# A transformer layer pair on one core: the first projections in two Strassen blocks per pair, and weight sums made by adding DMAs

## The chip, the cores and the metric

The kernel runs on one core of a Trainium2 chip (trn2). The metric is the device time of one launch in microseconds, lower is better. The kernel before takes 2067.45 us (median of three runs, 2067.3 to 2068.65).

## What is computed

Two transformer blocks over 256 tokens of width 2048, batch 1, all in float32. Cut to what matters here:

```python
h = rmsnorm(x, norm_mix_g)
proj = h @ w_in                        # 2048 x 6144: queries, keys, values, retention, its gate
x = x + concat(diff_attention(...), retention(...) * silu(rg)) @ w_o
x = x + cross_attention(rmsnorm(x, norm_x_g) @ w_xq, hm @ w_xk, hm @ w_xv) @ w_xo
x = x + (silu(hf @ w_gate) * (hf @ w_up)) @ w_down
# second block: h2 = rmsnorm(rmsnorm(x)) * (1 + scale) + shift, scale and shift from silu(c) @ w_ada
proj2 = h2 @ w_in_2                    # windowed attention, pooling, their gates
g = sigmoid(h2 @ w_merge + b_merge)
out = x + gate * rmsnorm((g_a * (y_a @ w_br_attn) + g_p * (y_p @ w_br_pool)) @ w_out)
```

## The kernel before

All large products have 256 tokens (two tiles of 128) on one side and a weight on the other. A **panel** is 512 columns of a weight. Its rows come in chunks of 512, each in two halves of 256 rows; a half (256 x 512, as 128 partitions x 1024 floats, 512 KB) is one **item**. An item is loaded by a DMA from SyncE's queue into one of eight places of `raw` (`RAWS = 8`). ScalarE then rounds it to float32r (`whi`, line 1718) and VectorE writes what the rounding left out (`wlo`, line 2494). TensorE multiplies with the activations, split in the same way, in three passes: high by high, high by low, low by high (lines 1117 to 1119), each one matmul of 128x128 stationary and 512 columns. One such split weight is an **entry**. Entries go through a ring of four (`HALVES = 4`): entry n is split when TensorE has finished entry n-4. A normal entry serves both token tiles and costs TensorE 12 matmuls.

Panels are worked on in **pairs** (f, s). The first 512 rows of a pair, called a block here, are done by Strassen's scheme in Winograd's form: seven products M1 to M7 in place of eight, each one token tile, so 6 matmuls. M5, M6, M7 and M4 need a sum or a difference of two items, which VectorE makes in place in `raw` (`sum_weights`, line 2507): M5 = b12 + b11, M6 = b22 + M5's sum, M7 = b11 - M6's sum, M4 = b21 + M6's sum. Activations are summed once per 512 rows (`make_forms`, lines 1819 to 1830). The panels of the first projection are named tq, v and rg; they meet the chunks x0 to x3 of x. After two single panels tq0 and tq1 come the five x pairs (v0, tq2), (tq3, v1), (tq4, tq5), (v2, rg0), (v3, rg1), then o, xk, xv, xq, xo; g with u, and d or e; kv alone; q with ga, pu with gp; m; ba, bp; out.

The order of everything is fixed when the program is built. `Stream` writes the list of steps, entries and items; `_slots` says how many entries are split before each step; `_loads` sorts the items by first use and gives each a place, the one whose last user comes soonest. SyncE issues the loads in that order, each waiting until its place is taken over by its last user. ScalarE and VectorE walk the same list of steps, and between entries take one piece of `jobs` (attention, norms, transposes) where a step allows it. GpSimd (POOL) issues the small loads and computes the roots of the norms (line 2547), strictly in the order of its program. `X`, 16 KB a partition, holds the rows of x: loaded at the start from POOL's queue (line 2579), squared by ScalarE for the norm (line 1148), and next used when `o` adds to it.

```python
for form, n in (("M5", at["M5"] - early), ("M6", at["M3"] + 1), ("M7", at["M1"] + 2),
                ("M4", max(at["M2"], at["M6"]) + 1)):
    self.sums_before[n] = at[form]     # before entry n is split, VectorE makes this sum
```

Of the kernel before, what the change touches and what calls it, by code (L numbers as in the profile page):

```python
# [9 lines left out]
F32 = mybir.dt.float32  # L10
F32R = mybir.dt.float32r
ALU = mybir.AluOpType
# [56 lines left out]
def layouts(v):  # L69
# [10 lines left out]
Entry = namedtuple("Entry", "item add minus nth")  # L80

Step = namedtuple("Step", "n p c hf tiles form start end made job taken snap aside")
# [8 lines left out]
FORMS = ("x", "mix", "mem", "hx", "xo", "hf", "h0", "h4", "h8", "mod", "mg")  # L91
TURNED = ("mix", "hx", "xo", "hf", "h0", "h4", "h8", "mg")

# [12 lines left out]
    "raw0", "raw1", "raw2", "raw3", "raw4", "raw5", "raw6", "raw7", "hi", "lo", "hi_first", "lo_first", "half", "t0_end", "ada",  # L106
# [12 lines left out]
    "x_hi", "x_lo", "mem_g", "mem_hi", "mem_lo", "st_hi", "a_hi", "a_lo", "af", "forms", "f_hi", "f_lo",  # L119

    "t_sum", "snap", "snap_v", "pre", "fin", "gated", "hh",
# [101 lines left out]
class Stream:  # L223
# [14 lines left out]
    def __init__(self, groups):  # L238
# [4 lines left out]
        self._done, self._set, self.sums = 0, 1, 0  # L243

        self.aside_at, self.ahead = {}, {}
        self.sums_before = {}
# [16 lines left out]
        self.last_of_item, self.last_sum_of = {}, {}  # L263
        for n, entry in enumerate(self.entries):
            self.last_of_item[entry.item] = n
            if entry.add is not None:
                self.last_sum_of[entry.add] = entry.nth
# [14 lines left out]
    def _entry(self, item, add=None, minus=False):  # L282
        if add is not None:
            self.sums += 1
        self.entries.append(Entry(item, add, minus, self.sums))
        return len(self.entries) - 1

    def _step(self, n, p, c, hf, tiles, form=None, start=False, end=False, job=True, taken=True, snap=None,
              aside=None):
        self.steps.append(Step(n, p, c, hf, tiles, form, start, end, None, job, taken, snap, aside))  # L290
        if end:
            self.end[p] = n + 1
# [21 lines left out]
    def _pair(self, f, s):  # L314
# [3 lines left out]
        b22, b12, b11, b21 = (self._item(*which) for which in ((f, 0, 1), (f, 0, 0), (s, 0, 0), (s, 0, 1)))  # L318
        todo = iter([(c, hf) for c in range(1, chunks) for hf in range(2)])
        at = {}  # L320
# [5 lines left out]
        def product(form, place, add=None, minus=False, **more):  # L326
            at[form] = n = self._entry(place, add, minus)
            panel, tile, _, half, _ = PRODUCTS[form]
            self._step(n, (f, s)[panel], 0, half, (tile,), form, **more)

        product("M5", b12, b11, start=True, job=False)
        product("M3", b22, start=True, job=False)
        normal(f, *next(todo), snap=("s5", q))
        product("M1", b11, start=True, job=False)
        if chunks == 4:
            normal(f, *next(todo), snap=("s1", q))
            product("M6", b22, b12)
            product("M2", b21, start=True, snap=("v", q))
            normal(f, *next(todo))
            normal(f, *next(todo))  # L340
        else:
            product("M2", b21, start=True, snap=("s1", q))
            product("M6", b22, b12)
            normal(f, *next(todo), snap=("v", q))
        product("M7", b11, b22, minus=True)
        normal(f, *next(todo), snap=("s3", q))
        product("M4", b21, b22, aside=q)
        for c, hf in todo:
            normal(f, c, hf)
        todo = {"u": self._early, "d": self._early, "m": self._late}.get(self.panels[s].kind, [])  # L350
        for i, (c, hf) in enumerate((c, hf) for c in range(1, chunks) for hf in range(2)):
# [3 lines left out]
        self.pairs.append(((f, s), at))  # L355

        early = 1 if self.panels[f - 1].stagger == "first" else 2
        for form, n in (("M5", at["M5"] - early), ("M6", at["M3"] + 1), ("M7", at["M1"] + 2),
# [2378 lines left out]
```

## Time and profile before

| | |
|---|---|
| runs, median of 3 | 2067.45 us |
| profiled execution, span | 2065.9 us |
| time around the span, as the median less the span | 1.5 us |
| TensorE busy, 9334 matmuls | 2054.4 us, 99% |
| VectorE / ScalarE / GpSimd busy | 1667.2 (81%) / 1181.2 (57%) / 50.0 us (2%) |
| TensorE in the chain that ended last | 95% |
| DMA engines, weight loads (queue q1) | 432.07 MB, 62.9% of their time |
| DMA engines, GpSimd's queue (q0) | 19.94 MB, 3.0% |
| granted TensorE clock | full in nearly all of the span |

The profiled execution has no time of its own beside its span. Busy shares are means over stages. A DMA's time "to landing" goes from its issue to the last of its sixteen signals. "Idle before" is an engine's own idle time ahead of an instruction, with what ended it. Matmuls overlap, so the mean duration of one (390 ns) is not the distance between two.

### The profile page before, as it was taken

What the parts mean: (1) busy time and instruction counts of PE and PEld (TensorE: products, weight loads), DVE (VectorE), ACT (ScalarE), POOL (GpSimd) and SP (SyncE); (2) the same over time, 40 slices, a digit from 0 to 9 for tenths busy, and PEclk for the clock granted to TensorE, in tenths of its full rate; (3) what the DMA queues carried; (4) which work ended last, traced back from release to release, by engine and by line L of the source; (5) the groups of instructions that cost most, each with busy time, mean ns of one, the idle gap of its engine ahead of it and who ended that gap; (6) DMA issues with size and microseconds to landing.
All of it is one profiled execution on the core that took longest, in us unless ns stands there. A gap on an engine that the chain in (4) does not pass through costs nothing.

```text
span 2065.9 us, 25348 instructions
## 1 busy us (share of the span) xinstructions
PE 2054.4 (99%) x9334; PEld 1699.8 (82%) x9334; DVE 1667.2 (81%) x1830; ACT 1181.2 (57%) x1533; POOL 50.0 (2%) x84
## 2 busy tenths in 40 slices
PE   9999999999999999999999999999999999999998
PEld 8888888888888888888888888888788888888787
DVE  6877778867766788989889898898777778988875
ACT  7666557656655565555555555555756655654453
POOL 1000000000000000000000000000000000000000
PEclk9999999999999999999999999999999999999999
DMA  9555557655544458777777777776465567789763
GB/s 347 180 172 184 184 180 259 225 182 184 189 158 153 159 185 300 267 259 242 243 237 259 261 242 243 236 270 213 158 214 178 180 201 234 269 285 329 219 197 109
DMA packets 219259, 453.74 MB, mean 220 GB/s; under 512 B 14449, under 2 KB 17153, under 8 KB 219009
## 3 DMA queue, kind: packets, MB, share of 16 engines
q1 hardware_dynamic: 213232, 432.07, 62.9%
q0 software_dynamic: 5616, 19.94, 3.0%
q8 instruction: 74, 1.21, 0.2%
q14 instruction: 49, 0.39, 0.1%
q10 hardware_dynamic: 288, 0.13, 0.0%
HBM read 447.88 MB, written 4.19 MB: 219 GB/s over the span
## 4 chain that ended last, share of the span: by engine, by line
PE 95%; DVE 2%; ACT 1%; issue 1%; DMA 1%; POOL 0%; SPq 0%; DVEq 0%; POOLq 0%; ACTq 0%
PE ps L1117 30%; PE ps L1119 30%; PE ps L1118 29%; PE ps L687 2%; DVE wlo L2494 1%; PE ps L837 1%; PE ps L817 1%; PE ps L921 0%; DMA FR<-in_post_norm_g_dram 0%; PE ps L952 0%; PE ps L963 0%; PE ps L901 0%; DMA FR<-in_x_t_dram 0%; ACT whi L1718 0%; DVE raw L2507 0%
## 5 line engine op out<-in xcount | busy, mean ns | idle before, releaser
L2494 DVE TENSOR_TENSOR wlo<-raw,whi 128x1024 fp32r<-128x1024 f32 x835 | 1010.4, 1222 | 262.8 <-ACT whi L1718 257.4
L1718 ACT ACTIVATE whi<-raw 128x1024 fp32r<-128x1024 f32 x835 | 876.6, 1058 | 564.5 <-PE ps L1119 518.2
L1117 PE MATMUL ps<-whi,bh 128*128 128x512 f32 x1384 | 547.3, 395 | 2.3 <-DVE wlo L2494 2.1
L1119 PE MATMUL ps<-whi,bl 128*128 128x512 f32 x1384 | 539.9, 390 | 0.0
L1118 PE MATMUL ps<-wlo,bh 128*128 128x512 f32 x1384 | 539.2, 390 | 0.0
L1117 PE MATMUL ps<-whi,ah 128*128 128x512 f32 x1080 | 429.3, 398 | 0.2 <-DVE wlo L2494 0.2
L1119 PE MATMUL ps<-whi,al 128*128 128x512 f32 x1080 | 421.6, 390 | 0.0
L1118 PE MATMUL ps<-wlo,ah 128*128 128x512 f32 x1080 | 420.9, 390 | 0.0
L1117 PEld LDWEIGHTS ps<-whi,bh 128*128 128x128 f32 x1384 | 260.1, 188 | 57.0 <-DVE wlo L2494 3.1
L1119 PEld LDWEIGHTS ps<-whi,bl 128*128 128x128 f32 x1384 | 259.8, 188 | 54.7
L1118 PEld LDWEIGHTS ps<-wlo,bh 128*128 128x128 f32 x1384 | 260.2, 188 | 52.5 <-issue 0.2
L1117 PEld LDWEIGHTS ps<-whi,ah 128*128 128x128 f32 x1080 | 202.9, 188 | 43.1 <-issue 1.3
L1119 PEld LDWEIGHTS ps<-whi,al 128*128 128x128 f32 x1080 | 202.8, 188 | 43.1
L1118 PEld LDWEIGHTS ps<-wlo,ah 128*128 128x128 f32 x1080 | 203.1, 188 | 41.5 <-issue 1.0
L2507 DVE TENSOR_TENSOR raw<-raw 128x1024 f32<-128x1024 f32 x160 | 195.6, 1223 | 15.7 <-DVE wlo L2494 15.7
L2108 DVE SCALAR_TENSOR_TENSOR FR<-raw,Z,FR 128x1024 f32<-128x1024 f32 x90 | 115.2, 1280 | 0.0
L1221 ACT ACTIVATE side<-ps 128x512 f32<-128x512 f32 x120 | 70.7, 589 | 16.3 <-PE ps L1119 16.3
L1117 PE MATMUL ps<-whi,fbh 128*128 128x512 f32 x184 | 73.9, 402 | 0.0
L1119 PE MATMUL ps<-whi,fbl 128*128 128x512 f32 x184 | 71.9, 391 | 0.0
L1118 PE MATMUL ps<-wlo,fbh 128*128 128x512 f32 x184 | 71.8, 390 | 0.0
L1835 DVE TENSOR_TENSOR FR<-ps,side 128x512 f32<-128x512 f32 x81 | 53.2, 685 | 7.7 <-PE ps L1119 7.7
L1117 PE MATMUL ps<-whi,fah 128*128 128x512 f32 x136 | 55.1, 405 | 0.0
(264 smaller groups left out, 1334.6 us busy)
## 6 DMA issues: line engine op xcount, KB each, us to landing
raw<-in_w_in_dram SPq DMA_DIRECT2D x168, 512.0 KB, 4.5
raw<-in_w_ada_dram SPq DMA_DIRECT2D x96, 512.0 KB, 4.6
raw<-in_w_gate_dram SPq DMA_DIRECT2D x88, 512.0 KB, 4.9
raw<-in_w_up_dram SPq DMA_DIRECT2D x88, 512.0 KB, 5.4
raw<-in_w_down_dram SPq DMA_DIRECT2D x88, 512.0 KB, 5.4
raw<-in_w_merge_dram SPq DMA_DIRECT2D x64, 512.0 KB, 5.0
raw<-in_w_o_dram SPq DMA_DIRECT2D x32, 512.0 KB, 4.8
raw<-in_w_xk_dram SPq DMA_DIRECT2D x32, 512.0 KB, 4.7
```

Source lines behind the costliest of these rows:

```text
L687: ins = e.transpose(T[b].ap[:, kk * 256 + t * 128:kk * 256 + t * 128 + 128], src[:, t, (2 * b + kk) * 128:(2 * b + kk + 1) * 128], ident[: ...
L817: ins = e.matmul(A[0].ap[:, t * S:(t + 1) * S], QTC[:, d, t * 128:(t + 1) * 128], XKT[:, 4 * h + d, :], start=(d == 0), stop=(d == 3))
L837: ins = e.matmul(A[b].ap[:, dd * S:(dd + 1) * S], XV[:, k, c0:c0 + 128], PTC[:, k, :], start=(k == 0), stop=(k == 1))
L1117: e.matmul(o, xh[:, k, tokens], wh, start=first, stop=False, skip_group_check=more)
L1118: e.matmul(o, xh[:, k, tokens], wl, start=False, stop=False, skip_group_check=more)
L1119: ins = e.matmul(o, xl[:, k, tokens], wh, start=False, skip_group_check=more, stop=kk == 1 and (st.end or st.form in READ))
L1221: done(e.activation(side_of(pair[place[0]], place[1]), bank_of(pair[panel], t)[:, :], ACT.Copy), "snap")
L1718: done(e.activation(split_at(n)[0], place(item), ACT.Copy), "hi")
L1835: return e.tensor_tensor(dst, src, side_of(p, t), side_op(p))
L2108: done(e.scalar_tensor_tensor(acc, src, csilu[:, k:k + 1], acc, ALU.mult, ALU.add), "ada")
L2494: done(e.tensor_tensor(lo, place(stream.entries[n].item), hi.bitcast(F32), ALU.subtract), "lo")
L2507: done(e.tensor_tensor(place(item), place(add), place(item), ALU.subtract if minus else ALU.add), "t_sum")
```

## The change

1. In the five x pairs two blocks (1024 of the 2048 rows) are done by Strassen's scheme (`QUADS`), with the products of both spread over the pair. Chunk x1 gets its own sums of activations (`x1`).
2. In the pairs named in `QUEUED` the sums are no longer VectorE's, but DMAs from GpSimd's queue that add one item to another in SBUF (`accum_op=ALU.add`, after.py line 2692): M5 and M4 of a pair with one block, M5, M6 and M4 of both blocks in the x pairs. Differences (M7), and all sums of g, u, d, e and m, stay on VectorE.
3. The table of places counts such a sum as in use for three entries longer (`LANDING = 3`).
4. From the end of tq1 to the end of rg1, `X` gives four more places (`SPARES = 4`); SyncE waits with the first of these loads until x has been squared, and x is loaded again before `o` needs it.

```diff
+QUADS = {"tq": 2, "v": 2, "rg": 2}
+QUEUED = ("tq", "v", "rg", "o", "xk", "xv", "xq", "xo", "q", "ga", "pu", "gp", "out")
+SPARES = 4
+LANDING = 3
...
+        else:
+            product("M5", 0, start=True, job=False)
+            product("M5", 1, job=False)
+            product("M3", 0, start=True)
+            normal(f, *next(todo), snap=("s5", q))
+            product("M3", 1, job=False)
+            product("M1", 0, start=True, job=False)
+            product("M1", 1)
             normal(f, *next(todo), snap=("s1", q))
...
+            product("M2", 0, start=True, job=False)
+            product("M6", 0)
+            product("M6", 1)
             normal(f, *next(todo), snap=("v", q))
...
+            product("M2", 1, job=False)
+            product("M7", 0)
+            product("M7", 1)
+            normal(f, *next(todo), snap=("s3", q))
+            product("M4", 0, aside=q)
...
             normal(s, c, hf)
...
+            if quads == 2 and i == 0:
+                product("M4", 1)
...
+        queued = self.panels[f].kind in QUEUED
+        early = 2
+        if self.panels[f - 1].stagger == "first":
+            early = 3 if queued else 1
+        elif queued:
+            early = 1 if q == 0 else 6
+        for k, made in enumerate(at):
+            for form, n in (("M5", made["M5"] - early), ("M6", made["M3"] + 1),
+                            ("M7", made["M1"] + 2 if quads == 1 else made["M6"] + 1),
+                            ("M4", max(made["M2"], made["M6"]) + 1)):
+                self.sums[made[form]] = Sum(n, made, k, form, queued and form in (("M5", "M4") if quads == 1 else ("M5", "M6", "M4")))
...
+        for m, one in self.sums.items():
+            for item in (self.entries[m].item, self.entries[m].add):
+                used(item, (one.before, 1))
+                used(item, (one.before + (LANDING if one.queue else 0), 1))
...
+        def ready_to_sum(e, m):
+
+            made, form = stream.sums[m].pair, stream.sums[m].form
+            if form == "M5":
+                for item in stream.entries[m]:
+                    e.wait_ge(*loaded(item))
+            else:
+                e.wait_ge(*sum_done(made["M5" if form == "M6" else "M6"]))
+                e.wait_ge(s["lo"], made[{"M6": "M3", "M7": "M1", "M4": "M2"}[form]] + 1)
...
+                while queued and stream.sums[queued[0]].before <= n:
+                    m = queued.pop(0)
+                    item, add = stream.entries[m]
+                    ready_to_sum(e, m)
+                    e.dma_start(place(item), place(add), accum_op=ALU.add).then_inc(sum_done(m)[0], 16)
...
+            add_weights(stream.end[index["rg", 1]] - 1)
+            for item in stream.last_in_spare.values():
+                wait_taken(e, item)
+            load_x()
...
+                elif stream.place[i] >= RAWS:
+                    e.wait_ge(s["x_sq"], 8)
```

`wait_taken` waits for the sums that read or write an item as well as for its last split. ScalarE waits for the sum's own signal before it splits the entry.

GpSimd's program at the start, from the root of the first norm (line 2547) and the load of the attention bias `c_bias` on. Before:

```order
L2547 TENSOR_TENSOR Z<-Z 128x2 [waits s_ms]
L2587 DMA FR<-in_c_bias_dram 128x1536
L2547 TENSOR_TENSOR Z<-Z 128x2 [waits s_ms] x4
```

and now:

```order
L2654 TENSOR_TENSOR Z<-Z 128x2 [waits s_ms]
L2712 DMA FR<-in_c_bias_dram 128x1536
L2692 DMA raw<-raw 128x1024 [waits s_raw0,s_raw7]
L2692 DMA X<-X 128x1024 [waits s_raw9,s_raw8]
L2692 DMA X<-raw 128x1024 [waits s_lo,s_sum_m5a]
L2692 DMA raw<-X 128x1024 [waits s_lo,s_sum_m5b]
L2692 DMA raw<-X 128x1024 [waits s_lo,s_sum_m6a]
L2692 DMA raw<-raw 128x1024 [waits s_lo,s_sum_m6b]
L2692 DMA X<-raw 128x1024 [waits s_raw7,s_raw11]
L2692 DMA raw<-X 128x1024 [waits s_raw8,s_raw3]
L2654 TENSOR_TENSOR Z<-Z 128x2 [waits s_ms]
```

The six sums of the first x pair (M5, M6, M4, each for both blocks) and the M5 of the next stand between the bias load and the next root; the first of them has the bias load ahead of it in the queue.

VectorE from the eviction of tq0 (line 1896 before, 2002 now) on, where the first x pair's M5 is made. Before:

```order
L1896 TENSOR_SCALAR FR<-ps,Z 128x512 [waits s_r,s_half]
L2507 TENSOR_TENSOR raw<-raw 128x1024 [waits s_raw7,s_raw6]
L2494 TENSOR_TENSOR wlo<-raw,whi 128x1024 [waits s_hi] x3
L1878 COPY FR<-ps 128x512 [waits s_t1_full]
L2494 TENSOR_TENSOR wlo<-raw,whi 128x1024 [waits s_hi]
```

and now:

```order
L2002 TENSOR_SCALAR FR<-ps,Z 128x512 [waits s_r,s_half]
L2604 TENSOR_TENSOR wlo<-raw,whi 128x1024 [waits s_hi] x3
L1984 COPY FR<-ps 128x512 [waits s_t1_full]
L2604 TENSOR_TENSOR wlo<-X,whi 128x1024 [waits s_hi]
```

The sum (line 2507) is gone from VectorE; its result is now waited for by ScalarE ahead of the third of these splits, and the M5 of the second block is the one read from `X`. Over the program TensorE has 8580 rows in place of 8610, VectorE 854 splits in place of 839 and 120 sums in place of 160, and GpSimd 60 adding DMAs.

## Rows read from the trace of the kernel before

**Rows 1.** The page: chain that ended last, by engine and by line.

```profile
PE 95%; DVE 2%; ACT 1%; issue 1%; DMA 1%; POOL 0%; SPq 0%; DVEq 0%; POOLq 0%; ACTq 0%
```

**Rows 2.** Waits of TensorE: us in total, times, longest.

```profile
PE ps L1117 <- DVE wlo L2494: 2.3, 4, 1.0
```

**Rows 3.** Timeline of TensorE, 540 to 548 us: start, duration; 37 matmuls.

```profile
539.67 0.39 PE L1119 MATMUL ps<-whi,al 128*128 128x512 f32 x1
...
547.83 0.39 PE L1119 MATMUL ps<-whi,al 128*128 128x512 f32 x1
```

**Rows 4.** Groups of instructions: the splits and the sums.

```profile
L2494 DVE TENSOR_TENSOR wlo<-raw,whi 128x1024 fp32r<-128x1024 f32 x835 | 1010.4, 1222 | 262.8 <-ACT whi L1718 257.4
L1718 ACT ACTIVATE whi<-raw 128x1024 fp32r<-128x1024 f32 x835 | 876.6, 1058 | 564.5 <-PE ps L1119 518.2
L2507 DVE TENSOR_TENSOR raw<-raw 128x1024 f32<-128x1024 f32 x160 | 195.6, 1223 | 15.7 <-DVE wlo L2494 15.7
```

**Rows 5.** Timeline of TensorE at the waits near 348 and 1504 us.

```profile
348.54 0.50 PE L1117 MATMUL ps<-whi,bh 128*128 128x512 f32 x1 [0.74 <-DVE wlo L2494]
...
1504.41 0.47 PE L1117 MATMUL ps<-whi,bh 128*128 128x512 f32 x1 [0.33 <-DVE wlo L2494]
```

**Rows 6.** The chain that ended last, same two places: start, us, what.

```profile
334.98 1.22 DVE raw L2507
...
1495.94 1.22 DVE raw L2507
```

**Rows 7.** The x pairs, 53 to 290 us: busy by engine, clock, DMA share.

```profile
53.00:290.00 237.00, 236.79 (x1092) 196.34 (x1091) 183.89 (x226) 144.23 (x212) 4.71 (x7) 1.00 0.58 184
```

**Rows 8.** DMA queues and issues in 53 to 290 us.

```profile
q1 hardware_dynamic: 22082, 42.57, 56.8%
...
raw<-in_w_in_dram SPq DMA_DIRECT2D x72, 512.0 KB, 4.3
```

**Rows 9.** All DMA issues from GpSimd's queue of 512 KB: median us to landing.

```profile
X<-in_x_dram POOLq DMA_DIRECT2D x4, 512.0 KB, 9.5
FR<-in_mem_t_dram POOLq DMA_DIRECT2D x4, 512.0 KB, 9.4
...
FR<-in_w_pool_group_dram POOLq DMA_DIRECT2D x2, 512.0 KB, 6.4
FR<-in_c_mg_dram POOLq DMA_DIRECT2D x2, 512.0 KB, 7.4
```

**Rows 10.** Line 2579, the four loads of x issued in a row.

```profile
DMA to landing us min/median/max: 7.6/9.5/11.5
```

**Rows 11.** Timeline of GpSimd, 20 to 43 us.

```profile
20.72 3.04 POOL L2579 DMA_DIRECT2D X<-in_x_dram  x4 [19.75 <-DMA raw<-in_w_in_dram]
...
41.37 0.73 POOL L2547 TENSOR_TENSOR Z<-Z 128x2 f32<-128x2 f32 x1 [13.90 <-DVE Z L1767]
42.06 0.60 POOL L2587 DMA_DIRECT2D FR<-in_c_bias_dram  x1
```

**Rows 12.** DMA queues, 46 to 48 us; then the issue of c_bias.

```profile
q0 software_dynamic: 112, 0.68, 83.8%
q1 hardware_dynamic: 80, 0.15, 19.9%
...
FR<-in_c_bias_dram POOLq DMA_DIRECT2D x1, 768.0 KB, 7.3
```

**Rows 13.** TensorE at the first x pair, its M5; ScalarE and VectorE on M5's split.

```profile
52.79 0.39 PE L1117 MATMUL ps<-whi,fah 128*128 128x512 f32 x1
...
45.26 1.05 ACT L1718 ACTIVATE whi<-raw 128x1024 fp32r<-128x1024 f32 x1
...
44.01 3.57 DVE L2494 TENSOR_TENSOR wlo<-raw,whi 128x1024 fp32r<-128x1024 f32 x3
```

**Rows 14.** Waits of VectorE in 53 to 290 us.

```profile
DVE wlo L2494 <- ACT whi L1718: 30.9, 33, 1.7
...
DVE FR L2012 <- POOL Z L2547: 3.3, 4, 0.9
```

More of the change, by code:

```diff
@@ L77 @@
 Panel = namedtuple("Panel", "kind i w col rows stagger")
-Entry = namedtuple("Entry", "item add minus nth")
-Step = namedtuple("Step", "n p c hf tiles form start end made job taken snap aside")
+Entry = namedtuple("Entry", "item add")
+Step = namedtuple("Step", "n p c hf tiles form quad start end made job taken snap aside")
+Sum = namedtuple("Sum", "before pair quad form queue")
+Spare = namedtuple("Spare", "first last")
 PRODUCTS = {"M3": (0, 0, True, 1, 0), "M5": (0, 1, True, 1, 1), "M1": (1, 1, False, 0, 0),
@@ L266, in __init__ @@
             if entry.add is not None:
-                self.last_sum_of[entry.add] = entry.nth
+                self.sums_of.setdefault(entry.add, []).append(n)
+        self.sum_order = sorted(self.sums, key=lambda m: self.sums[m].before)
+        self.sum_signal, used = {}, {}
+        for m in self.sum_order:
+            one = self.sums[m]
+            name = f"sum_{one.form.lower()}{'ab'[one.quad]}" if one.queue else "sum_w"
+            used[name] = used.get(name, 0) + 1
+            self.sum_signal[m] = name, used[name] * (16 if one.queue else 1)
+        self.spares = [Spare(self.end_of["tq", 1], self.end_of["rg", 1])] * SPARES
         self._places()
@@ L346, in _pair, with product @@
[L346 to L349, printed above, removed]
+        def product(form, k, start=False, **more):
+            b22, b12, b11, b21 = places[k]
+            item, add = {"M5": (b12, b11), "M3": (b22, None), "M1": (b11, None), "M6": (b22, b12), "M2": (b21, None),
+                         "M7": (b11, b22), "M4": (b21, b22)}[form]
+            at[k][form] = n = self._entry(item, add)
+            panel, tile, _, half, _ = PRODUCTS[form]
+            self._step(n, (f, s)[panel], k, half, (tile,), form, k, start=(start and k == 0), **more)
@@ L1729, in scalar_program @@
                 jobs.start(job)
+            for job in (pause(8), make_forms("x1")):
+                aside.start(job)
             for i, st in enumerate(stream.steps):
@@ L1823, in make_forms @@
                 after_own(done(e.tensor_tensor(a11, a22, a11, ALU.subtract)))
[L1824 removed]
+                done(e.tensor_tensor(a12, a12, a11, ALU.add), summed)
                 yield
@@ L2489, in make @@
                         add_ada(item)
-                    if n in stream.sums_before:
-                        sum_weights(stream.sums_before[n])
+                    for m in [m for m in stream.sum_order if stream.sums[m].before == n and not stream.sums[m].queue]:
+                        sum_weights(m)
                     hi, lo = split_at(n)
@@ L2496, in sum_weights @@
             def sum_weights(n):
[L2498 to L2507 removed]
+                item, add = stream.entries[n]
+                ready_to_sum(e, n)
+                done(e.tensor_tensor(place(item), place(add), place(item),
+                                     ALU.subtract if stream.sums[n].form == "M7" else ALU.add), "sum_w")
             done(e.memset(tbl[:, :], 0.0), "tbl_zero")
@@ L2517, in vector_program @@
                 jobs.start(job)
+            for job in (pause(8), make_forms("x1")):
+                aside.start(job)
             for i, st in enumerate(stream.steps):
```

202 lines of the change are left out of this document (121 added, 81 removed).

## The prediction

> **What bounds the kernel now.** I read the chain that ended last first: TensorE holds 95% of it [rows 1]. Then what TensorE waits for: VectorE's splits, four times, 2.3 us in all [rows 2]. So the time is the number of matmuls times the distance between two. The timeline gives that distance: 37 matmuls start within 547.83 - 539.67 = 8.16 us, so 0.227 us each at the full clock [rows 3]. A product (6 matmuls) is 1.36 us of TensorE, a normal entry (12) 2.72. VectorE and ScalarE have room: both wait for the ring before a split, VectorE 262.8 us in all and ScalarE 564.5 [rows 4]. In the x pairs VectorE is busy 184 of 237 us and still waits 30.9 us for ScalarE's halves of the splits [rows 7, 14]. The DMA engines are busy 58% there [rows 7]. A matmul less is therefore worth its full 0.227 us; a sum less on VectorE is worth something only where TensorE waits for it; and a new wait costs only what is left of it after the ring of four entries has run empty.
>
> **Matmuls, certain.** Each x pair does seven products for eight once more: 6 matmuls less, 5 pairs, 30 in all, which is what TensorE's rows say (8610 to 8580). 30 x 0.227 = **-6.8 us**. The clock stays full, since TensorE stays busy.
>
> **Splits and sums.** 15 more entries cost ScalarE 15 x 1.06 and VectorE 15 x 1.22 us, and 40 sums less give VectorE 40 x 1.22 back [rows 4]. In the x pairs the balance on VectorE is 15 x 1.22 - 10 x 1.22 = +6.1 us over some 230 us, beside 53 us in which it was idle [rows 7]: that costs nothing as long as the ring hides it (below). In the other stages 30 sums leave VectorE. That gains where a sum stood in the chain. Two of TensorE's waits qualify: at 348.54 (0.74 us) and at 1504.41 (0.33 us) [rows 5]; each chain goes back through VectorE without a gap worth naming to an M5 sum (334.98, 1495.94) [rows 6], which takes 1.22 us, more than either wait. Both M5 move to the queue with several entries of lead. **-1.1 us.** The other waits come from the norm between the layers and stay.
>
> **The x1 forms** (4 scalings, 4 small sums, one split on each side) run between entries of tq1, where TensorE does not wait. Nothing; without cover some 3 us of VectorE would be late once.
>
> **The adding DMAs.** No row shows one. Nearest are GpSimd's loads of the same size: medians 6.4 to 9.5 us to landing [rows 9], 7.6 when first and 11.5 when last of four in a row [rows 10]. Below: how much data moves per time. In 46 to 48 us queue q0 alone took 83.8% of the engines for 0.68 MB, so 0.52 MB takes 0.838 x 2 x 0.52/0.68 = 1.3 us of all sixteen [rows 12]. If the sum reads its target too, twice that, 2.6. An estimate for a lone sum is 6.4 to 9.5 plus 0 to 1.3, so 6.4 to 10.8, middle 8 us. The Trainium skill says why reading might count double: an adding transfer issues two source reads per chunk on the same ring, and its rate halves (Collectives: The Full Stack, The bandwidth ceiling); no row here can show it.
>
> What the program allows: the second block's M6 sum is asked for when that block's M3 is split. From the moment M3's slot is free (TensorE has finished the entry four before it) until TensorE starts M6 there are 7 products and 2 normal entries, 7 x 1.36 + 2 x 2.72 = 15.0 us. Off go 2.3 us for M6's own split (as for the first M5, from 45.26 to 44.01 + 3.57 = 47.58 [rows 13]) and 2.6 for M3's, the same and 0.3 for the signals. That leaves **10.1 us**. The same sum for the second M4, and for M4 in pairs with one block, leaves 11.4; the first block's M6 has 12.8. M5 has six entries of lead. So a sum of 8 us is hidden; only the far end of the range, or a burst like the four loads, is not.
>
> The load on the DMA engines: q1 took 56.8% of 237 us for 42.57 MB [rows 8]. The 30 sums of the x pairs add 39 to 78 us to 137, so a share of 0.75 to 0.92. Loads land in 4.3 us [rows 8]; they get slower, but are due 7 us or more ahead of use by the table, with four more places. Nothing in the sum; up to 3 us in the range.
>
> Here a rule speaks. The skill's fit for a DMA from GpSimd's queue is 2.0 us plus bytes / 436e3 (DMA: Bandwidth & Descriptors, Anatomy of one DMA): 3.2 us for one item. The rows say 6.4 and more for the same size, so the trace disagrees and I don't use it. By the page no sum could be late, and the result would be the best case below.
>
> **The first x pair, the place that costs.** Its M5 has no lead. GpSimd works in order: root at 41.37, c_bias at 42.06 to 42.66 [rows 11], then M5 of block one. c_bias lands at 42.06 + 7.3 = 49.4 [rows 12], and the sum's data follow it on the same queue. TensorE starts that M5 at 52.79 [rows 13]; VectorE's sum was done nearly 9 us before [rows 13]. The second sum follows on the queue at once, if its two items (which wait for x to be squared, about 41 us) are there by then. Bounds: each takes 1.3 us after the one ahead (landing 50.7 and 52.0), or, at the pace of the four x loads in the same rush, (11.5 - 7.6)/3 + 0.73 = 2.0 us doubled for the second read (53.4 and 57.4). I take 2.6 us, the data rate above with two reads: 52.0 and 54.6. The split adds 2.3. So the first M5 is ready at 54.3, 1.5 us late; the second at 56.9 where TensorE comes free at 54.3 + 1.36 = 55.7, 1.2 late. **+2.7 us** (low 0.2, high 5.6). Behind ScalarE's wait stand its evictions and snapshots, which nobody needs sooner.
>
> **Products in a row.** Before, three entries in a row always held a normal one, 5.44 us; now M3 M1 M1, M2 M6 M6 and M2 M7 M7 take 4.08. A split takes 2.6 us from a free slot to ready, so 1.5 us is left for jobs in between, and a job's burst on VectorE is 2 to 3 us. Each such place can cost 0 to 1 us, 15 to 20 places; most are caught up by the normal entry ahead. I take **+1.0 us** in all, bounds 0 and 4.
>
> **Moved waits.** x is reloaded (2 MB, 4 issues of 0.73 us each) when the last spare place is free, some 20 us ahead of `o`'s first use and 11.5 us long at worst [rows 10]: hidden. Roots: VectorE waits for one 3.3 us over four heads [rows 14]; an issue of a sum ahead of it adds 0.7 at most, in VectorE's slack.
>
> **Sum.** -6.8 - 1.1 + 2.7 + 1.0 = -4.2 us. Against the profiled span that is 2065.9 - 4.2 = 2061.7; the median of the runs stands 1.5 us over that span, so **2063.2 us** against 2067.45. A measurement can tell about 0.2% of this kernel, 4.1 us, from no change; the forecast lies just at that edge, on the side of faster.
>
> **The rivals.**
> *A, the forecast or better:* 2063.2, down to 2067.45 - 6.8 - 1.1 + 0.2 = 2059.7 if the sums are cheap and nothing is late. For it: TensorE is the bound, and the matmuls are gone for certain. Chance 0.44.
> *B, paid back in place:* the first pair costs its high end, 5.6, and the rows of products 2 us: 2067.45 - 7.9 + 7.6 = 2067.1. For it: c_bias is ahead of the sums, and the engines are full when they come, 83.8 and 19.9% [rows 12]. Chance 0.34.
> *C, slower: sums land behind their window in every x pair.* Decisive is the landing of the second block's M6: above 10.1 us ScalarE's wait empties the ring, and each us over is one of TensorE's, for M6 and, above 11.4, again for M4. At 12.8 us (11.5 as in rows 10, plus a second read of 1.3) that is 2.7 + 1.4 = 4.1 us per pair, 20.5 in five; with the first pair's 5.6 and 1.0 for products 2067.45 - 7.9 + 27.1 = 2086.7; at 11.4 us 6.5 + 5.6 + 1.0 - 7.9, so 2072.7. For it: queue q0 was never used beside busy loads in this stage but for single transfers, and the engines go from 58 to 75 or 92%. Against it: lone transfers land in 6.4 to 7.4. A way to get there is GpSimd itself, which would have to issue while VectorE works 78% of the time. The four x issues took 3.04 us, 0.76 each, and c_bias 0.60 [rows 11], so no row shows a hold-up. The skill says that VectorE with two inputs in SBUF contends with GpSimd's reads, but not with the writing of descriptors (SBUF — State Buffer, Who interferes with whom); by that, the trace agrees and this way is closed. Chance 0.22.
> That the matmuls aren't saved is excluded by the rows of TensorE.
>
> **How the numbers follow.** Faster by over 0.2% (below 2063.3) is A: 0.44. Within 0.2% (2063.3 to 2071.6) is B with the mildest part of C: 0.34. Slower is the rest of C: 0.22. The range starts at 2059, just under the best case, and reaches into C to 2075, a landing near 11.6 us; beyond it lies some 0.15. The own range of A and B is 2059.5 to 2068.
>
> **What will show it.** The three matmul lines count 30 less. TensorE waits near 53 and 56 us for wlo, 1.5 and 1.2 us; the waits at 348 and 1504 are gone. The adding DMAs show 6.4 to 10.8 us to landing, q0's share grows by 60 x 1.3 to 2.6 us, 4 to 8% of the span, and ScalarE waits for them in few places. Wrong would be: TensorE waits for VectorE in every x pair by more than 1 us (C), no wait at 53 us (A's best case), or sums that take over 12 us.

## The result, and the profile after

The changed kernel takes 2082.81 us (median of four runs, 2082.58 to 2086.58) against 2067.95 of the kernel before in the same session: a ratio of 1.0074, 95% interval [1.0062, 1.0086]. It is slower by 15 us, beyond the range of the forecast (2059 to 2075). Its profiled execution has a span of 2080.6 us, 14.7 over that of before. Two kernels below (e9 and e12) each had one execution far out of line (3470 and 7460 us, with a granted clock of 0.56 and 0.27), from which nothing is read.

The page of the changed kernel, busy time and chain; the groups that answer to [rows 1, 4] (splits L2604 and L1818):

```profile
PE 2052.0 (99%) x9304; PEld 1693.9 (81%) x9304; DVE 1642.5 (79%) x1810; ACT 1198.7 (58%) x1553; POOL 105.4 (5%) x148
...
q1 hardware_dynamic: 213232, 432.07, 61.4%
q0 software_dynamic: 14832, 53.50, 11.8%
...
PE 90%; DVE 4%; ACT 2%; issue 2%; DMA 2%; SPq 0%; POOL 0%; DVEq 0%; POOLq 0%; ACTq 0%
```

TensorE lost its 30 matmuls (9334 to 9304 records), VectorE has less to do, and yet TensorE's share of the chain falls from 95 to 90%. Its waits, against 2.3 us for VectorE's splits [rows 2]:

```profile
PE ps L1213 <- issue: 6.5, 2, 3.8
PE ps L1213 <- DVE wlo L2604: 4.8, 5, 1.7
PE ps L1213 <- DVE side L1961: 2.8, 3, 1.4
PE ps L1213 <- ACT side L1318: 2.8, 2, 2.3
PE ps L782 <- ACT FR L1307: 2.0, 2, 1.1
PE ps L1154 <- POOL ones L2648: 1.0, 1, 1.0
PE ps L845 <- DVE FR L2110: 0.8, 1, 0.8
```

**Where the time went.** TensorE's matmuls of lines 1213 to 1215 run in the order of the program, so the start of each panel can be compared with that of the kernel before. This table has the difference in us (positive: later than before) for this and all kernels below, each from one profiled execution. A step from one column to the next is what that stretch cost; "a pair costs" means such a step below, and the first pair's goes from tq1 to tq3, because a late M5 already delays the start of v0. Two executions of one kind differ by some 0.5 us at the start. The five x pairs lie between v0 and o0 (v0, tq3, tq4, v2 and v3 are their first panels, o0 the panel behind them); each should have given 1.36 us.

```
                              tq1   v0  tq3  tq4   v2   v3   o0  xk0  xk2  ga0   end
the change                    1.4  5.3 11.1 11.8 12.8 14.6 14.5 13.5 16.2 15.3  14.7
e1_first_m5_vector            1.5  1.5  2.4  3.1  4.1  5.9  5.8  4.8  8.8  8.0   7.3
e2_one_block                  0.5  5.2 10.5 10.5 10.5 10.5 10.5  9.6 13.8 12.9  12.2
e3_sums_on_vector             1.7  1.7  3.0  7.5 10.9 15.2 19.5 19.5 19.5 19.6  19.4
e4_mem_ahead                  1.8  5.8 13.1 13.8 14.8 16.7 16.5 15.5 17.0 16.1  16.2
e5_copy_not_add               2.1  5.3 11.5 12.2 13.2 15.0 14.9 13.9 14.3 13.6  12.9
e6_bias_behind                1.6  4.1 12.9 13.5 14.6 16.4 16.3 15.3 19.5 18.7  18.0
e7_loads_held                 1.8  1.7  7.9  8.6  9.6 11.4 11.3 10.3 12.8 12.1  11.9
e8_three_mended               0.4  0.4  2.0  2.7  3.7  5.6  5.5  4.4  6.3  5.4   4.8
e9_difference_first           0.1  0.1  1.7  1.6  1.5  3.3  2.1  1.1  3.1  2.2   1.6
e10_m7_later                  0.7  0.7  2.3  3.0  4.4  8.0  7.9  6.9  8.8  7.9   7.3
e11_both                      0.1  0.1  1.7  1.5  1.9  2.6  1.4  0.4  2.1  1.2   0.7
e12_one_block_mended          0.9  0.9  0.9  0.9  1.0  1.0  1.0 -0.0  1.6  0.7   0.0
e13_two_blocks_xk_vector      0.1  0.0  1.6  1.5  1.9  2.6  1.3  0.3  0.3 -0.6  -1.2
e14_one_block_xk_vector       0.2  0.1  0.2  0.2  0.2  0.2  0.2 -0.8 -0.8 -1.4  -2.0
e15_two_blocks_last_pair      0.2  0.1  0.4  0.4  0.5  0.5 -0.2 -0.5 -0.5 -1.3  -2.0
e16_two_blocks_no_landing     0.2  0.2  1.7  1.6  2.0  3.5  2.3  1.3  2.8  1.9   1.3
```

In the change 1.4 us go at the start, 9.7 in the first x pair (that is 11.1 with the 1.36 it should have given), 3.4 in the other four (8.9 with theirs), 2.7 between xk0 and xk2; 1.0, 0.9 and 0.6 us come back at three places (in o, up to the q pairs, before out).

A step of this table holds both TensorE's waits and what the clock took behind them, and the second differs from execution to execution. For the first pair the two can be told apart (waits in 50 to 72 us; granted clock as the mean over 57 to 71 us; the clock's price is an estimate, half of TensorE's busy time while the granted clock was at half, 1.2 GHz). That price is part of the first column:

```
                            pair costs   waits   clock 57-71   price of the clock
the change                        9.7     6.8      0.88          1.4
e1_first_m5_vector                0.9     0.0      1.00          0.0
e2_one_block                     10.0     6.3      0.76          3.4
e4_mem_ahead                     11.3     6.2      0.63          4.0
e5_copy_not_add                   9.4     4.9      0.76          3.4
e6_bias_behind                   11.3     4.5      0.51          5.8
e7_loads_held                     6.1     3.2      0.88          1.7
```

**The first pair.** TensorE there, the last matmul before the gap and those behind it (start, duration, idle before):

```profile
53.93 0.39 PE L1215 MATMUL ps<-whi,al 128*128 128x512 f32 x1
58.07 0.77 PE L1213 MATMUL ps<-whi,fah 128*128 128x512 f32 x1 [3.75 <-issue]
...
60.34 0.63 PE L1215 MATMUL ps<-whi,fal 128*128 128x512 f32 x1
61.31 0.47 PE L1213 MATMUL ps<-whi,bh 128*128 128x512 f32 x1 [0.34 <-DVE wlo L2604]
...
65.66 0.47 PE L1213 MATMUL ps<-whi,fah 128*128 128x512 f32 x1 [2.72 <-issue]
```

and ScalarE, which waits for the two M5 sums:

```profile
55.66 1.06 ACT L1818 ACTIVATE whi<-raw 128x1024 fp32r<-128x1024 f32 x1 [9.38 <-DMA raw<-raw]
58.85 1.06 ACT L1818 ACTIVATE whi<-X 128x1024 fp32r<-128x1024 f32 x1 [2.14 <-DMA X<-X]
61.62 0.20 ACT L1420 ACTIVATE Z<-Z 128x2 f32<-128x2 f32 x1 [1.72 <-DVE Z L2077]
61.85 1.28 ACT L1422 ACT_TABLE_LOAD   x1
...
63.26 1.04 ACT L1818 ACTIVATE whi<-X 128x1024 fp32r<-128x1024 f32 x1
```

The sums were issued at 43.61 and 47.60 us and landed 12.0 and 11.2 us later. The releaser "issue" of TensorE's two long waits says only that the profile inferred none; ScalarE's rows give it. The first wait is for the sum. The second (2.72 us, at 65.66) is for the next split, which ScalarE begins at 63.26 because one of its jobs, waiting for VectorE, stands between it and the sums' splits. The windows say why the sums were late (behind the five engines' busy times, PE, PEld, DVE, ACT, POOL: granted clock, DMA share, GB/s). Before:

```profile
50.00:54.00 4.00, 4.00 (x20) 3.30 (x19) 2.80 (x7) 3.57 (x6) 0.00 (x0) 1.00 0.33 124
54.00:58.00 4.00, 4.00 (x19) 3.31 (x18) 4.00 (x5) 3.01 (x4) 0.00 (x0) 1.00 0.80 257
58.00:62.00 4.00, 4.00 (x21) 3.33 (x20) 2.76 (x4) 2.98 (x4) 0.00 (x0) 1.00 0.44 137
```

and now:

```profile
50.00:54.00 4.00, 4.00 (x20) 3.23 (x18) 0.00 (x0) 0.00 (x0) 0.00 (x0) 1.00 1.03 263
54.00:58.00 4.00, 0.32 (x2) 0.00 (x0) 1.26 (x2) 1.06 (x1) 0.00 (x0) 0.94 1.05 264
58.00:62.00 4.00, 3.59 (x9) 2.46 (x10) 2.36 (x7) 1.41 (x3) 0.00 (x0) 0.63 1.05 404
...
53.00:290.00 237.00, 221.59 (x1003) 179.52 (x1002) 184.20 (x234) 156.28 (x223) 30.01 (x36) 0.99 0.86 244
```

In 50 to 54 us the DMA engines were at 0.33 and are now full, as they are from 44 to 65 us. SyncE issues nine loads in 42 to 49 us, the first four into the new spare places; before it issued three in 40 to 47. With c_bias and two sums that read and write, all of it stands in line: c_bias lands at 52.8 us (before: 49.4), the sums 2.9 and 6.1 us behind it. Over the five pairs the share rose from 0.58 [rows 7] to 0.86, inside the 0.75 to 0.92 forecast; in this stretch the mean says nothing.

### The profile page after: what moved, and what is told of

Read it like the earlier page. It is cut to its first block, busy times and chain, and to the rows that moved or that the text cites. A ratio compares the mean times of both kernels' runs of the same rounds, so it can differ in the third digit from the quotient of the medians.

```text
span 2080.6 us, 25310 instructions
## 1 busy us (share of the span) xinstructions
PE 2052.0 (99%) x9304; PEld 1693.9 (81%) x9304; DVE 1642.5 (79%) x1810; ACT 1198.7 (58%) x1553; POOL 105.4 (5%) x148
## 3 DMA queue, kind: packets, MB, share of 16 engines
q0 software_dynamic: 14832, 53.50, 11.8%
## 4 chain that ended last, share of the span: by engine, by line
PE 90%; DVE 4%; ACT 2%; issue 2%; DMA 2%; SPq 0%; POOL 0%; DVEq 0%; POOLq 0%; ACTq 0%
PE ps L1213 28%; PE ps L1215 28%; PE ps L1214 28%; DVE wlo L2604 2%; PE ps L782 2%; ACT whi L1818 1%; PE ps L932 1%; PE ps L912 1%; ACT junk L1244 1%; DMA X<-X 1%; DMA FR<-in_mem_dram 1%; DMA FR<-in_x_t_dram 0%; PE ps L1016 0%; PE ps L1058 0%; PE ps L1047 0%
## 5 line engine op out<-in xcount | busy, mean ns | idle before, releaser
L2604 DVE TENSOR_TENSOR wlo<-raw,whi 128x1024 fp32r<-128x1024 f32 x811 | 979.9, 1220 | 300.4 <-ACT whi L1818 295.6
L1818 ACT ACTIVATE whi<-raw 128x1024 fp32r<-128x1024 f32 x811 | 850.6, 1057 | 556.0 <-PE ps L1215 481.8
L1213 PE MATMUL ps<-whi,bh 128*128 128x512 f32 x1424 | 563.3, 396 | 1.5 <-DVE wlo L2604 1.4
L1215 PE MATMUL ps<-whi,bl 128*128 128x512 f32 x1424 | 555.1, 390 | 0.0
L1214 PE MATMUL ps<-wlo,bh 128*128 128x512 f32 x1424 | 554.4, 389 | 0.0
L1213 PE MATMUL ps<-whi,ah 128*128 128x512 f32 x1030 | 409.8, 398 | 6.3 <-DVE wlo L2604 3.5
L1215 PE MATMUL ps<-whi,al 128*128 128x512 f32 x1030 | 401.8, 390 | 0.0
L1214 PE MATMUL ps<-wlo,ah 128*128 128x512 f32 x1030 | 401.1, 389 | 0.0
L2610 DVE TENSOR_TENSOR raw<-raw 128x1024 f32<-128x1024 f32 x114 | 139.2, 1221 | 5.5
L2692 POOL DMA_DIRECT2D raw<-raw x43 | 38.5, 910 | 597.1 <-DVE wlo L2604 539.3
```

What stands on the lines that cost most here:

```text
L1213: e.matmul(o, xh[:, k, tokens], wh, start=first, stop=False, skip_group_check=more)
L1214: e.matmul(o, xh[:, k, tokens], wl, start=False, stop=False, skip_group_check=more)
L1215: ins = e.matmul(o, xl[:, k, tokens], wh, start=False, skip_group_check=more, stop=kk == 1 and (st.end or st.form in READ))
L1818: done(e.activation(split_at(n)[0], place(item), ACT.Copy), "hi")
L2604: done(e.tensor_tensor(lo, place(stream.entries[n].item), hi.bitcast(F32), ALU.subtract), "lo")
L2610: done(e.tensor_tensor(place(item), place(add), place(item), ALU.subtract if stream.sums[n].form == "M7" else ALU.add), "sum_w")
```

## The experiments

Each kernel is compared with the kernel before on the same chip; ratios have their 95% interval. Diffs are against the changed kernel.

### The first pair's sums on VectorE

```diff
-  Sum(n, made, k, form, queued and form in (("M5", "M4") if quads == 1 else ("M5", "M6", "M4")))
+  Sum(n, made, k, form, queued and form in (("M5", "M4") if quads == 1 else ("M6", "M4") if q == 0 else ("M5", "M6", "M4")))
```

> The M5 sums of both blocks of the first x pair are VectorE's again; the other 58 adding DMAs stay. Theory 1 (the first pair is late because its sums stand behind c_bias and beside a rush of loads, landing 55.6 and 58.8 us): TensorE starts M5 near 53 us again, the waits of 3.8 and 2.7 us at 58 and 66 us shrink, and the run is 6 to 9 us faster, 2074 to 2077. Rival 2 (the row of three products with jobs between them costs the first pair its 11 us whatever makes the sums): the waits only move, less than 3 us is gained, over 2080.

2075.22 us, 1.0033 [1.0021, 1.0044], as theory 1 had it: 7.6 us of the 15 are two DMAs. The first pair costs 0.9 us in place of 9.7, the wait of 3.75 us is gone, and from tq3 on the table runs 8.7 us below that of the change, up to xk0. The 4.0 us between xk0 and xk2 are no worse a wait than in the change (2.0 us against 2.3): the granted clock fell to half behind it, 0.89 in 405 to 420 us against 1.00.

### One block only

```diff
-QUADS = {"tq": 2, "v": 2, "rg": 2}
+QUADS = {}
```

The scaling and the sums of x1 go too.

> One block per x pair as before, without the x1 forms; sums of M5 and M4 still by adding DMAs, places counted as in the change. 30 matmuls come back (+6.8 us). Theory 1 (late sums in the first pair, and the mem loads queued behind a sum at xk0 for 2.7 us): one late M5 costs 3 to 5 us, xk0 costs 2.7, the vanished waits give 2, so 2070 to 2073. Rival 2 (products in a row): the first pair costs nothing, 2067 to 2069. Rival 3 (the adding DMAs slow everything by contention): over 2076.

2079.05 us, 1.0056 [1.0041, 1.0071] (the profiled execution, the table's, took 2081.01). Above what theory 1 gave, and not for the reason of rival 3: the first pair costs 10.0 us with a single late sum, the other four cost exactly nothing (10.5 in five columns). TensorE's waits:

```profile
57.97 0.47 PE L1213 MATMUL ps<-whi,fah 128*128 128x512 f32 x1 [4.54 <-issue]
64.33 0.50 PE L1213 MATMUL ps<-whi,ah 128*128 128x512 f32 x1 [1.77 <-DVE wlo L2599]
```

The loss is thus not Strassen's second block but the first sum's landing at 55.5 us, the same as in the change. I had put too low what a late M5 costs: behind it stand ScalarE's jobs and evictions, so a second wait follows 6 us later, and the granted clock fell to half behind each of the two, which took 3.4 of the 10.0 us.

### No adding DMAs at all

```diff
-QUEUED = ("tq", "v", "rg", "o", ...)
+QUEUED = ()
```

> Two blocks, all 120 sums on VectorE, no adding DMA. Theory 1: the first pair's 11 us and xk0's 2.7 are gained back, but VectorE takes 30 sums of 1.22 us more in the x pairs (about 226 of 230 us busy), so TensorE waits for it there at many places: 2075 to 2090, with the panel after the first pair at least 5 us earlier than in the change. Rival (the adding DMAs are the whole loss and VectorE has room): 2060 to 2066.

2088.86 us, 1.01 [1.0085, 1.0115], theory 1. The first pair costs 1.3 us, but each later one 3.4 to 4.5 (the last with some 1.6 us at half clock). The windows of 53 to 290 us and TensorE's waits:

```profile
53.00:290.00 237.00, 219.14 (x985) 175.96 (x984) 207.28 (x247) 150.43 (x217) 4.71 (x7) 0.99 0.54 171
```

```profile
PE ps L1213 <- DVE wlo L2604: 10.3, 14, 1.8
PE ps L1213 <- DVE side L1961: 7.6, 4, 2.8
```

VectorE is busy 207 of 237 us (184 before, [rows 7]) and TensorE waits for it 18 times. The adding DMAs are what makes two blocks bearable in pairs two to five; what they cost they cost in the first, and 2.7 us at xk0.

### Is it the second read?

```diff
-  e.dma_start(place(item), place(add), accum_op=ALU.add)...
+  e.dma_start(place(item), place(add))...
```

> The 60 DMAs copy one item over the other in place of adding it: the output is not the reference's, the transfers have one read less. Theory 2R (an adding DMA reads its target too): queue q0 falls from 11.8% to about 6.8% of the engines' time (1.3 us of all sixteen per item in place of 3.05), landings fall from a median of 6.7 by 1 to 2 us, the first pair's sums land 3 us sooner, and the run is at 2076 to 2080. Rival (the price is the queue's and the SBUF to SBUF transfer's, not the addition's): q0 stays over 10%, and the time stays within 2 us of 2082.8.

2080.31 us (two runs), 1.006 [1.004, 1.008]. This kernel leaves out the addition, so its output isn't the layer's. The landings of these 60 DMAs in the change, then in this run, and the queue in this run:

```profile
DMA to landing us min/median/max: 4.6/6.7/14.2
```

```profile
DMA to landing us min/median/max: 2.8/4.8/11.3
```

```profile
q0 software_dynamic: 14832, 53.50, 7.3%
```

The queue without any sum (the run before this one) takes 3.3%, so 60 adding DMAs took (11.8 - 3.3)% x 2080.6 us / 60 = 2.9 us of all sixteen engines each, and 60 copies (7.3 - 3.3)% x 2078.8 us / 60 = 1.4: the addition doubles the price. It is only a part of what made the first pair late. The first copy landed at 55.65 us, as the sum had at 55.63 (issued 0.7 us later), the second at 57.64 in place of 58.83: in a full stretch what stands ahead in line weighs more than the price of the transfer. TensorE's waits in the first pair fell from 6.8 to 4.9 us, but the clock took that back, and the pair cost 9.4 us as against 9.7. What is gained in this execution, 2.3 us, lies between xk0 and xk2 (0.4 in place of 2.7).

### c_bias, or the rush of loads?

```diff
+  add_weights(stream.sums[stream.pairs[0][1]["M5"]].before)
   e.dma_start(CB, a["c_bias"])...
```

> c_bias is issued behind the two M5 sums of the first x pair, in place of ahead of them. Theory 1a (c_bias, 0.79 MB, is what holds them): M5 of the first block lands 2 to 3 us sooner than 55.6 and the panel v0 starts 2 to 3 us sooner. Theory 1b (the rush of nine loads of SyncE, issued in 42 to 49 us and landing one each 1.35 us, is what holds them): under 1.5 us.

2084.37 us (2081.74 to 2085.69), 1.0077 [1.0062, 1.0092]. The sum landed at 54.40 in place of 55.63 and v0 starts 1.2 us sooner: theory 1b. The loads behind the sums land where they did, the last at 66.8 us against 66.6, and c_bias only at 60.3. TensorE's waits in the pair fell from 6.8 to 4.5 us, and yet it costs 11.3. The profiled execution took 2085.69, and its granted clock stayed at half from 57 to 71 us (behind the busy times: clock, DMA share, GB/s; the change, then this run):

```profile
57.00:71.00 14.00, 9.87 (x39) 7.33 (x40) 10.39 (x19) 9.45 (x13) 1.70 (x2) 0.88 0.86 261
```

```profile
57.00:71.00 14.00, 11.85 (x30) 8.40 (x30) 9.00 (x17) 9.15 (x12) 1.69 (x2) 0.51 0.96 308
```

So the 11.3 us say nothing against moving c_bias; the runs show no gain either.

```diff
   elif stream.place[i] >= RAWS:
       e.wait_ge(s["x_sq"], 8)
+      if stream.place[i] >= RAWS + 2:
+          e.wait_ge(*sum_done(stream.pairs[0][1]["M5"]))
```

> As the run before, and SyncE's third load into a spare place (and so all behind it) waits until the second M5 sum has landed. Theory 1b: the engines are free for the sums, which land within 7 us of their issue, the first near 50, the second near 54, and v0 starts within 2 us of its time before (52.8); but seven loads start some 8 us later and land from 56 to 66, so the panel tq2 is still 5 to 10 us late. Theory 1a: nothing beyond what the move of c_bias gave.

2079.86 us, 1.006 [1.0043, 1.0077]. ScalarE's waits for the two sums:

```profile
50.07 1.06 ACT L1818 ACTIVATE whi<-raw 128x1024 fp32r<-128x1024 f32 x1 [3.44 <-DMA raw<-raw]
53.57 1.06 ACT L1818 ACTIVATE whi<-X 128x1024 fp32r<-128x1024 f32 x1 [2.44 <-DMA X<-X]
```

With the loads out of the way the sums land in 6.4 and 5.6 us and v0 starts on time; then the loads held back are late (a wait of 3.2 us at 60.8), and tq3 starts 7.9 us late all the same. So the rush was the main cause of the late sums (moving c_bias alone gave 1.2 us), and there is no room in this stretch for both: from 46 us on the DMA engines have work without a gap in either order.

### The queue of GpSimd, at xk0

In the change GpSimd waits at the M4 sum of (xk0, xk1), with two loads of mem and a root behind it; before, these loads went out at 385.9 and 389.7 us (GpSimd's timeline of the change, then ScalarE's):

```profile
401.93 0.84 POOL L2692 DMA_DIRECT2D raw<-raw  x1 [32.62 <-DVE wlo L2604]
402.54 1.73 POOL L2737 DMA_DIRECT2D FR<-in_mem_dram  x2
```

```profile
411.89 0.63 ACT L1244 ACTIVATE junk<-FR 128x512 bf16<-128x512 f32 x1 [4.62 <-DMA FR<-in_mem_dram]
```

TensorE then waits 2.33 us for ScalarE at 417.33. The edit moves `add_weights(entry_of("xk", 0, 4))` behind these loads.

> GpSimd issues the last two loads of mem before it waits for the M4 sum of (xk0, xk1). Theory 1 (in-order queue: the loads stand behind that wait until 401.9 us, and TensorE waits 2.3 us for what comes of them): the panels from xk2 on start 2.5 us earlier than in the change, all before it unchanged, 2080.3. In the one-block run the same place costs 4.1 us. Rival (the landing is slow because of the adding DMAs themselves, whatever the order): less than 1 us.

2084.4 us, 1.0082 [1.0067, 1.0097]: no gain in the time. The first pair cost 11.3 us in this execution against 9.7, with shorter waits and a lower clock (0.63 against 0.88 in 57 to 71 us), which hides it; at its own place the table says 1.5 in place of 2.7. Half the expected gain, because the sum now waits behind the second load, which itself waits for a square of ScalarE, and ScalarE stands 3.62 us for the sum.

```diff
-QUEUED = (..., "o", "xk", "xv", ...)
+QUEUED = (..., "o", "xv", ...)
```

on top of the mended kernels with two blocks and with one (below):

> The best two-block version so far, with the sums of the xk pairs on VectorE. If the M4 sum's place in GpSimd's queue is what is left at xk0, the panels from xk2 on come 1.7 us sooner: 2067.9. If mem itself is late, nothing changes: 2069.6.

> The mended one-block version with the sums of the xk pairs on VectorE: 2068.2 less 1.6 is 2066.6 by the queue's place, 2068.2 by the rival.

2066.99 us (0.9996 [0.9987, 1.0005]) and 2065.85 us (0.9991 [0.9982, 1.0]), both 0.8 to 0.9 us under what was expected; from xk0 to xk2 both cost 0.0. So the whole loss here came from the sums in GpSimd's queue.

### The rest of the x pairs

Three edits together: the first pair's M5 on VectorE, mem ahead of the sum, and x1 scaled by a job of its own:

```diff
+            def scale_x1():
+                for k in range(4):
+                    ins = e.activation(AF["x1"][:, k, :], XT[1][:, k, :], ACT.Copy, scale=gcols("mix", 1)[k])
+                    if k == 1:
+                        yield
+                done(ins, "af")
+                yield
...
-            for job in (pause(8), make_forms("x1")):
+            for job in (pause(6), scale_x1(), make_forms("x1")):
```

> Three edits at three places: the first pair's M5 sums by VectorE, mem loads ahead of the sum, the scaling of x1 as a later job of ScalarE in two pieces. They should add up: 2075.2 (the first alone) less 4 at xk0 (which had 4.0 there in that run) less 1.3 at the start, 2070. If the first pair's jobs swallow the start's gain, 2071.5.

2073.23 us, 1.0025 [1.0016, 1.0035], above the 2070 to 2071.5 expected: 1.1 at the start, and 2.1 at xk0 of the 4 hoped for. Of these 2.1, 1.7 are the half clock that the trace of e1 had there and this one has not. With this edit tq1 starts 0.1 to 0.7 us late in all seven two-block kernels that have it, without it 1.4 to 2.1 in seven. Left are pairs that cost 1.6, 0.7, 1.0, 1.9 and -0.1 us where each should give 1.36. Two orders of VectorE in them, apart and together: the difference for tile 1 (line 1961) ahead of the splits of its step, and each M7 sum later:

```diff
-  read_first = st.snap and st.snap[0] == "v" and len(panels[st.p].rows) == 3
+  read_first = st.snap and st.snap[0] == "v" and (len(panels[st.p].rows) == 3 or panels[st.p].kind in QUADS)
```

```diff
-  ("M7", made["M1"] + 2 if quads == 1 else made["M6"] + 1),
+  ("M7", made["M1"] + 2 if quads == 1 else made["M7"] - 1),
```

> The three mended places, and in the x pairs VectorE reads the difference for tile 1 ahead of the splits of that step, as pairs with three chunks have it. Theory D (VectorE's order costs the two-block pairs: TensorE waits 2.8 us, 3 times, for that difference): those waits go, the splits behind it come 0.7 us later each and cost at most 1 us, 2070.5 to 2071.5 against 2073.2. Rival (VectorE is simply late there and the order only moves the wait): 2072.5 to 2074.

> The three mended places, and each M7 sum stands right ahead of the split that comes before its own, in place of both ahead of the normal entry behind M2 M6 M6. Theory D: the normal entry's split comes up to 2.4 us sooner, TensorE's waits for wlo fall from 3.8 to about 1.5 us, 2071. Rival (M2 M7 M7 are as dense and become late in its place): 2073 or more.

> Both edits of VectorE's order. If they add: 2068.5 to 2070. If the four-deep ring and the rows of three products set the loss whatever the order: over 2072.

2070.13 (1.0009 [1.0, 1.0019]), 2075.29 (1.004 [1.0025, 1.0054]) and 2069.56 us (1.0009 [0.9999, 1.0018]). The first is 0.4 us under its range, the third within. The second is a miss, on the rival's side: its waits for wlo fell from 3.8 to 1.2 us, but those for the difference rose from 2.8 to 6.2, because a sum moved later stands ahead of it; the longest of these waits also brought some 1.6 us at half clock, at 229 us (line 1961 is 1967 here, 2604 is 2610):

```profile
PE ps L1213 <- DVE side L1967: 6.2, 4, 2.8
...
PE ps L1213 <- DVE wlo L2610: 1.2, 2, 1.0
```

Both together, the difference is safe again and a little is gained. TensorE's waits of that run:

```profile
PE ps L1213 <- DVE side L1967: 2.3, 2, 1.6
PE ps L782 <- ACT FR L1307: 2.0, 2, 1.1
PE ps L1213 <- ACT side L1318: 1.6, 2, 1.3
...
PE ps L845 <- DVE FR L2116: 0.8, 1, 0.8
```

Against it, one block with the first M5 on VectorE and mem ahead of the sum:

> One block, the first M5 on VectorE, mem loads ahead of the sum; all other M5 and M4 by adding DMAs. Theory: nothing of the two blocks is left, so 2067.9 less 2.0 for the vanished waits plus some 2 at xk0, 2067 to 2068.5; then two blocks, mended, cost 5 us more than one in spite of 6.8 us of matmuls saved. Rival (the adding DMAs slow the x pairs too): over 2070.

2068.23 us, 1.0 [0.999, 1.0009], as expected. From tq1 to o0 the table holds still: with one block the pairs give what they gave before. And two blocks where the mended two-block version gained, in (v3, rg1) alone, with the mends and orders above and the xk sums on VectorE ("the run before" is the one-block kernel with these, 2065.85 us):

```diff
-        quads = min(QUADS.get(self.panels[f].kind, 1), chunks - 1)
+        quads = 2 if (self.panels[f].kind, self.panels[f].i) == ("v", 3) else 1
```

> As the run before, with two blocks in the last x pair (v3, rg1) alone, the one where the mended two-block version gained 1.2 us. If a pair without a pile of VectorE's jobs keeps its 1.36 us: 1.2 less than the run before, 2065.4, the best of all. If a row of products costs its gain wherever it stands: equal to the run before or up to 1 us over it.

2066.3 us, 0.9994 [0.9985, 1.0003], against 2065.85 with no second block. In its profile that pair gives 0.7 us of its 1.36; in the runs nothing can be seen of it, which is the second of the two expectations. At last the table of places:

```diff
-LANDING = 3
+LANDING = 0
```

> The mended two-block version with LANDING = 0 in place of 3: places are counted as free at the sum's own time, so SyncE's loads are given other places, and some wait for a sum to land. Theory (the table's constant has no part in the loss; the loads are early anyway): 2069.6 within 1.5 us. Rival (without it SyncE stands at places that a sum still holds, and loads come late in the x pairs): over 2072.

2069.63 us (2068.77 to 2075.35), 1.0016 [1.0007, 1.0025], against 2069.56 (2068.23 to 2071.38) with 3: by the median no part in the loss. Three of its ten runs took over 2073 us, and no trace shows them.

## Why the prediction was wrong

In the forecast's own terms the 14.7 us of the two profiles are -6.8 (matmuls), -2.5 (old waits), some +8.5 (first pair), +11.5 (products in a row), +1.4 (x1 forms and start) and +2.7 (moved waits). Two terms failed: the products in a row, 11.5 for 1.0, and the first pair, 8.5 for 2.7.

- **Matmuls, -6.8 us.** The 30 are gone. That this is worth its full price rested on "TensorE is the bound", which holds only while the ring stays full; the runs with one and two blocks mended alike (2065.85 and 2066.99) show that in the x pairs all of it goes into waits, and 1 us more.
- **The two old waits, -1.1.** Right in place, and low: 1.0 us came back in o, 0.9 from xk2 up to the q pairs, and 0.6 before out. The best kernel of all, with one block, has these alone: 2.0 us under before, half of what a measurement can tell.
- **The adding DMAs' price.** 2.9 us of all sixteen engines lies near the 2.6 with two reads; the median landing of 6.7 us lies at the low end of 6.4 to 10.8. The second block's M6, the number that was to decide, landed in 5.6 to 7.2 us, well inside its window of 10.1. (The share of 0.75 to 0.92 was added up a little wrong: 176 and 215 of 237 us are 0.74 and 0.91.) The Trainium skill's rule that an adding transfer issues two reads per chunk and halves its rate (Collectives: The Full Stack, The bandwidth ceiling) agrees with the trace: 2.9 against 1.4 for the copy. The Trainium skill's fit of 2.0 us plus bytes / 436e3 (DMA: Bandwidth & Descriptors, Anatomy of one DMA) gives 3.2 us; no sum landed under 4.6, and the plain copies of e5 had a median of 4.8, the quickest 2.8.
- **The first x pair, +2.7 (0.2 to 5.6): a step that failed.** I let c_bias land at 49.4, where the kernel before had it, and the sums follow at 2.6 us each, to 52.0 and 54.6. They landed at 55.6 and 58.8. The pace was nearly right (2.9 and 3.2 us); c_bias itself landed 3.4 us late, at 52.8, and that is what carried the sums out of the range. The load on the engines was taken from a mean over 237 us and from 2 us of the kernel before, in which SyncE had few places to load into. The change itself adds four, so nine loads start in the same 7 us; I counted the bytes of the sums there, but not the loads that the new places bring forward. I also took a late M5 as lateness alone. Behind it came a second wait of 2.72 us, and the clock, which I had called full and which took 1.4 us more. It measured 8 to 9 us: 11.1 less the 2.3 to 3.0 that the pair costs with VectorE's M5 sums (0.9 and 1.6 in the table, with 1.36 not gained).
- **Products in a row, +1.0 (0 to 4): mis-sized, and the largest error.** 11.9 us in the mended kernel (5.1 from tq1 to o0, and 6.8 not gained), 8.1 with VectorE's order mended too. I counted only the ring's time from a free slot to a ready split, and left out the row M5 M5 M3. VectorE's difference, which a product waits for, and its M7 sums, two of which stand ahead of one split, were not in the sum; nor that TensorE's small matmuls (transposes, attention) then wait for ScalarE and VectorE (2.0 and 0.8 us). The distances between the starts of TensorE's matmuls in e11, less those of the kernel before, divide the 8.1: 3.3 us at these small matmuls, 3.1 where a product waits until VectorE has read a difference or ScalarE has copied a bank aside, 0.6 in one wait at 56 us, and 1.1 in waits too short for the rows and in small matmuls. (A wait costs about 0.2 us more than its row says, because matmuls overlap: from 53.93 to 58.07 us are 4.14, less 0.23 for the matmul 3.91, against 3.75 in the row.)
- **The x1 forms, 0.** They cost 1.2 us: eight scalings of ScalarE in one piece delay the split of entry 6, for which TensorE waits 1.22 us at 25.89.
- **Moved waits, 0.** Wrong by 2.7 us. I looked at the reload of x and the roots, not at mem's loads, which stood behind a sum that waits for a split.
- **The rivals.** C gave 2072.7 to 2086.7, and the time lies there, but by another way: its decisive number, a landing of M6 over 10.1 us, did not come about, and VectorE's splits held TensorE 5 times, not twice a pair. So that the time fell into C's range is luck. B had the right place, the first pair, and two thirds of its price.

## What to carry to other kernels

A transfer without lead must be costed against what the DMA engines do in those very microseconds, in the kernel as changed: list the loads that new places bring forward, and add up the line. A queue in program order makes every wait in it a wait for all that stands behind. And a saved matmul is gained only if the engines that feed it can follow the denser order; count all they do per product, not the splits alone. Last, before two executions are compared stretch by stretch, take the clock out: here it took 1.4 to 5.8 us in one and the same stretch, and hid a gain in the waits.

## What the runs showed of the hardware

- The sum's issue took GpSimd 0.86 us, the copy's 0.53 (medians, same size).
- The granted clock fell to half, 1.2 GHz, near the end of TensorE's idle 3.75 us (from 54.3 to 58.07): 0.76 in 57 to 58 us, 0.50 from 58 to 60, 0.53 in 60 to 61, then full. The six matmuls from 58.07 on stand 0.43 us apart (the first two 0.56) in place of 0.227, which adds about 1.4 us to a wait of 3.75. How long it stayed low differed: in e6 (waits of 2.3, 0.7 and 1.5 us) it was 0.51 in 57 to 71 us. What decides that, no run here shows.
- Loads of 512 KB landed 1.35 us apart while the engines were full (59.9, 61.3, 62.6, 64.0 us in the change; 60.3, 61.5, 62.8, 64.2 in e6).
